# A three-block transformer kernel: merged orders in latent and memory attention, boundary sums of the last two tiles on TensorE

## The reference, cut to what matters

```python
# first block (x: 512 x 1024, mem: 256 x 1024)
y = hybrid_mixer(rms_norm(x, g1))                       # convolution + forgetting attention
x = x + rms_norm(y, g2)                                 # norm 1
q, k, v = rms_norm(x, g3) @ w_mq, mem_n @ w_mk, mem_n @ w_mv   # 4 heads of 128
y = (softmax(q @ k.T * 128 ** -0.5) @ v) @ w_mo         # memory attention
x = x + rms_norm(y, g4)                                 # norm 2
y = square(relu(rms_norm(x, g5) @ w_up)) @ w_down
x = x + rms_norm(y, g6)                                 # norm 3
# second block, two layers
c_q, c_kv, k_rope = split(x @ mla_w_in, [384, 256, 64])
q = rms_norm(c_q, g_q) @ w_uq                           # 8 heads, 128 plain + 64 rotated
k, v = split(rms_norm(c_kv, g_kv) @ w_ukv)
m = attention(q, k, v, rope) @ w_o                      # latent attention
x = layer_norm(alpha * x + m)                           # layer norm 1
x = layer_norm(alpha * x + conv_ffn(x))                 # layer norm 2
x = layer_norm(alpha * x + hyena_mixer(x))              # layer norm 3
x = layer_norm(alpha * x + conv_ffn(x))                 # layer norm 4, the output
```

## Time and profile before

| what | value |
|---|---|
| three runs | 2267.39, 2268.22, 2272.98 us |
| median | 2268.22 us |
| profiled execution | 2269.26 us |
| its span | 2267.5 us |
| mean granted TensorE clock | 0.949 of full speed |
| busy PE, DVE, POOL, ACT | 93%, 58%, 42%, 37% |

### The profile page before, as it was taken

The page is one execution under the profiler, slowest core; times in us unless marked ns, Lnnn a source line. Parts: engine busy times, 40 slices in busy tenths (PEclk is TensorE's granted clock), DMA queues, the critical chain, the costliest instruction groups (busy, mean ns, idle before and its releaser), DMA issues.

```text
span 2267.5 us, 23112 instructions
## 1 busy us (share of the span) xinstructions
PE 2113.5 (93%) x9481; PEld 1718.9 (76%) x9481; DVE 1323.7 (58%) x1597; ACT 840.9 (37%) x1194; POOL 941.4 (42%) x388
## 2 busy tenths in 40 slices
PE   8999989779999998899989999999988789999997
PEld 5777768668888886677778887877877677887786
DVE  7765871625234443455177776546578827777644
ACT  4623454453122224467143333223322324333322
POOL 4252145535444445111444444444666434444442
PEclk9998869889999998999989999999999989999998
DMA  5322112112232221111212222224231222222221
GB/s 196 136 97 74 38 38 89 62 54 75 97 108 93 93 93 54 40 48 38 75 56 95 104 98 93 93 74 160 91 129 52 110 73 75 93 96 98 104 93 38
DMA packets 34558, 194.02 MB, mean 86 GB/s; under 512 B 3903, under 2 KB 4495, under 8 KB 14932
## 3 DMA queue, kind: packets, MB, share of 16 engines
q1 hardware_dynamic: 34452, 192.54, 24.5%
HBM read 178.82 MB, written 13.64 MB: 85 GB/s over the span
## 4 chain that ended last, share of the span: by engine, by line
PE 61%; DVE 24%; ACT 10%; POOL 3%; issue 2%; DMA 0%; SPq 0%; DVEq 0%; POOLq 0%; ACTq 0%
PE ps L128 55%; DVE TMP L157 9%; DVE TMP L163 6%; PE ps L127 5%; ACT WH L144 4%; DVE TMP L151 1%; ACT TMP L145 1%; DVE X L151 1%; ACT PAD L144 1%; PE ps L136 1%; POOL X L151 1%; DVE ps L163 1%; DVE VG L151 1%; POOL WL L151 1%; POOL TMP L151 1%
## 5 line engine op out<-in xcount | busy, mean ns | idle before, releaser
L151 POOL TENSOR_TENSOR WL<-W,WH 128x2048 fp32r<-128x2048 f32 (+3 forms) x175 | 705.6, 4037 | 1036.4 <-ACT WH L144 1036.4
L128 PE MATMUL ps<-HH,WL 128*128 128x512 f32 x1456 | 583.9, 401 | 48.4 <-issue 15.6
L128 PE MATMUL ps<-HL,WH 128*128 128x512 f32 x1456 | 575.4, 395 | 0.0
L128 PE MATMUL ps<-HH,WH 128*128 128x512 f32 x1456 | 574.5, 395 | 0.0
L144 ACT ACTIVATE WH<-W 128x2048 fp32r<-128x2048 f32 (+2 forms) x157 | 291.8, 1859 | 322.5 <-PE ps L128 322.5
L128 PEld LDWEIGHTS ps<-HH,WL 128*128 128x128 f32 x1456 | 278.8, 192 | 120.8 <-issue 53.1
L128 PEld LDWEIGHTS ps<-HH,WH 128*128 128x128 f32 x1456 | 278.5, 191 | 60.2
L128 PEld LDWEIGHTS ps<-HL,WH 128*128 128x128 f32 x1456 | 279.0, 192 | 56.3 <-issue 0.2
L151 DVE TENSOR_TENSOR MRL<-MID,MRH 128x512 fp32r<-128x512 f32 x76 | 177.4, 2366 | 162.4 <-ACT MRH L144 162.4
L157 DVE TENSOR_SCALAR TMP<-PAD,PAR 128x512 f32<-128x512 f32 x88 | 209.0, 2375 | 69.9 <-ACT PAD L144 69.9
L128 PE MATMUL ps<-MRH,WL 128*128 128x512 f32 x608 | 238.3, 392 | 4.5 <-DVE TMP L163 2.3
(11 more groups left out here) (338 smaller groups left out, 3162.0 us busy)
## 6 DMA issues: line engine op xcount, KB each, us to landing
W<-in_up SPq DMA_DIRECT2D x44, 1024.0 KB, 4.8
W<-in_down SPq DMA_DIRECT2D x22, 1024.0 KB, 4.8
W<-in_w_up SPq DMA_DIRECT2D x16, 1024.0 KB, 4.8
W<-in_w_down SPq DMA_DIRECT2D x16, 1024.0 KB, 4.8
W<-in_hy_in SPq DMA_DIRECT2D x12, 1024.0 KB, 4.8
kd<-STG SPq DMA_DIRECT2D x36, 256.0 KB, 2.0
KB<-kd SPq DMA_DIRECT2D x8, 1024.0 KB, 5.1
W<-in_win_ag SPq DMA_DIRECT2D x4, 1024.0 KB, 4.8
```

The source lines that it names most:

```text
L128: return self.eng.matmul(out, lhs, rhs, start=start, stop=stop)
L151: return QUIET if self.eng is None else self.eng.tensor_tensor(out, a, b, op)
```

## The change

Memory attention: a second pair of buffers for the turned tiles; the heads overlap more in all three engines' lists; DVE does two of the four scalings. Latent attention: the sums of c_q and their spread come earlier in the input projection, the root and the high parts with them; low parts are made one tile late, so that the next scaling is not held up; the key/value scale is spread between query tiles; the swap stands ahead of the keys. Norms: POOL adds squares 0 to 5, and TensorE sums DG, square 6 and square 7; in norms 1 to 3 the scaled tiles 0 and 1 go to a PSUM bank (`yp`) instead of Y. Layer norms: the order of the sums is DG, square 6, X 7, square 7; HH 0 comes first and X 0 is scaled by DVE, which also makes HL 0; POOL makes HL 2, 4 and 5; mean and multiplication are interleaved between tiles. In layer norm 4 POOL subtracts and multiplies tiles 6 and 7 from copies of the two banks that ACT makes.

```diff
--- before.py
+++ after.py
@@ -339,8 +339,8 @@
...
         PM = [sb(f"PM{i}", A + (72, 88)[i], [128, 4, 256]) for i in range(2)]
-        PMH = sb("PMH", A + 92, [128, 2, 512], R)
-        PML = sb("PML", A + 96, [128, 2, 512], R)
+        PMH = [sb(f"PMH{i}", A + (92, 76)[i], [128, 2, 512], R) for i in range(2)]
+        PML = [sb(f"PML{i}", A + (96, 80)[i], [128, 2, 512], R) for i in range(2)]
         OMH = sb("OMH", A + 100, [128, 4, 512], R)
@@ -518,8 +518,8 @@
...
                                 ins = step(ps, m, k, wh, wl)
-                                if within and k == KT // 2:
-                                    within(g)
+                                if within:
+                                    within(g, k)
                             ins.then_inc(*up(acc, (group, g), *[("w_used", n)] * (m == MT - 1)))
@@ -719,7 +719,10 @@
...
             def post(s, name):
-                column_sum([(("ys", s), DG, ("yacc", s, 6), None, None),
+                reserve("yp", s)
+                close("yp", s)
+                column_sum([(("ys", s), DG, ("yacc", s, 5), None, None),
+                            (("ys", s), tmp(name, 6), ("ysq", s, 6), (name, 6), None),
                             (("ys", s), tmp(name, 7), ("ysq", s, 7), (name, 7), ("ys", s))])
@@ -775,7 +778,8 @@
...
                     pe.wait_ge(*at("vm", j))
-                    ins = pe.mm3(ps[:], VMH[:, j, blk(h)], VML[:, j, blk(h)], PMH[:, j, :], PML[:, j, :], j == 0, j == 1)
+                    ins = pe.mm3(ps[:], VMH[:, j, blk(h)], VML[:, j, blk(h)], PMH[h % 2][:, j, :], PML[h % 2][:, j, :],
+                                 j == 0, j == 1)
                 ins.then_inc(*up(acc, ("mo", h)))
@@ -785,13 +789,16 @@
...
             mem_t(0)
+            mem_s(2)
             mem_q(3)
-            for h in range(4):
-                if h < 2:
-                    mem_s(h + 2)
-                mem_pv(h)
-                if h < 3:
-                    mem_t(h + 1)
+            mem_t(1)
+            mem_pv(0)
+            mem_s(3)
+            mem_t(2)
+            mem_pv(1)
+            mem_pv(2)
+            mem_t(3)
+            mem_pv(3)
@@ -841,11 +848,11 @@
...
-            def within_in(n):
-                if n == 4:
+            def within_in(n, k):
+                if (n, k) == (4, 3):
                     column_sum([(("cqs",), DG, ("cqadd", 1), None, None),
                                 (("cqs",), tmp("cq", 2), ("cqsq", 2), ("cq", 2), ("cqs",))])
-                if n == 5:
+                if (n, k) == (5, 0):
                     spread("nq", slot=12)
@@ -864,6 +871,8 @@
...
                     ins.then_inc(*up(acc, ("uq", p, m), *[("w_used", n)] * (m == 2)))
+                    if p == 0 and m == 1:
+                        spread("nv", slot=20)
@@ -925,7 +934,6 @@
...
             mla_uq(0)
-            spread("nv", slot=20)
             swap_q(0)
@@ -936,8 +944,8 @@
...
                     mla_uq(p + 1)
+                    swap_q(p + 1)
                     mla_k(p + 1)
-                    swap_q(p + 1)
                 mla_t(2 * p + 1)
@@ -956,7 +964,9 @@
...
                 ds, dq = ("ds", d), ("dq", d)
-                column_sum([(ds, X[:, 7, :], ("cx", d, 7), None, ds), (dq, DG, ("qacc", d, 6), None, None),
+                column_sum([(dq, DG, ("qacc", d, 5), None, None),
+                            (dq, tmp("dc", d, 6), ("dcq", d, 6), ("dc", d, 6), None),
+                            (ds, X[:, 7, :], ("cx", d, 7), None, ds),
                             (dq, tmp("dc", d, 7), ("dcq", d, 7), ("dc", d, 7), dq)])
@@ -1354,7 +1364,7 @@
...
-                for i in range(4):
+                for i in range(2):
                     s, p = 32 * (h % 2) + 168 + i, PM[h % 2][:, i, :]
@@ -1362,9 +1372,9 @@
...
                     act.wait_ge(*at("mt", h, j))
-                    if h:
-                        act.wait_ge(*at("mo", h - 1))
-                    high(PMH[:, j, :], bank("mt", h, j)[:], ("pm", h, j))
+                    if h >= 2:
+                        act.wait_ge(*at("mo", h - 2))
+                    high(PMH[h % 2][:, j, :], bank("mt", h, j)[:], ("pm", h, j))
@@ -1379,15 +1389,18 @@
...
             mem_norm(1)
+            mem_exp(2)
             mq_high(3)
-            for h in range(4):
-                if h < 2:
-                    mem_exp(h + 2)
-                mem_out(h)
-                if h < 3:
-                    mem_turned(h + 1)
-                if h < 2:
-                    mem_norm(h + 2)
+            mem_norm(2)
+            mem_turned(1)
+            mem_out(0)
+            mem_exp(3)
+            mem_turned(2)
+            mem_norm(3)
+            mem_out(1)
+            mem_out(2)
+            mem_turned(3)
+            mem_out(3)
             roots_next()
@@ -1457,14 +1470,17 @@
...
                         act.copy(KRS[:], bank("mi", 0)[:]).then_inc(*out(("krs",)))
+                    if m == 3:
+                        root(("cqs",), 8, "eps6")
                     if m == 4:
-                        root(("cqs",), 8, "eps6")
-            for k in range(3):
-                q_high(k)
+                        q_high(0)
+                        q_high(1)
+            q_high(2)
+            weights(CH["uq"][0])
             root(("cvs",), 16, "eps6")
-            weights(CH["uq"][0] + 1)
             act.wait_ge(*at("rkt"))
             high(KRH[:], AN2[:], ("kr",))
+            weights(CH["uq"][0] + 1)
@@ -1489,11 +1505,11 @@
...
-            nope(0)
             query(0)
...
                 high(CVH[:, k, :], tmp("nv", k)[:], ("cvn", k))
+            nope(0)
@@ -1558,8 +1574,17 @@
...
                 act.act(SM[:, 24:28], SM[:, 24:28], ACT.Sqrt, 1.0, par("eps5")).then_inc(*out(("sd", d)))
+                if not split:
+                    act.wait_ge(*at("mu", d))
+                    act.copy(RS[:], bank("mu", d)[:]).then_inc(*out(("mus",)))
+                    act.wait_ge(*at("rstd", d))
+                    act.copy(DG[:], bank("rstd", d)[:]).then_inc(*out(("rstds",)))
                 for k in range(8):
                     act.wait_ge(*at("xn", d, k))
+                    if split and k == 0:
+                        act.act(HH[:, 0, :], X[:, 0, :], ACT.Identity, par(g), par(b)).then_inc(
+                            *out(("hn", 4 + d, 0, "hi")))
+                        continue
                     if split:
@@ -1955,16 +1980,22 @@
...
             def post(s, Y, g, g2):
+
                 inverse(("ys", s), 8, [("col", "rps", s)])
+                dve.wait_ge(*at("free", *earlier["yp", s]))
                 for k in range(10):
                     if k < 8:
+                        yn = Y[:, k, :] if k > 1 else bank("yp", s)[:]
                         dve.wait_ge(*at("rps", s))
                         dve.wait_ge(*at("y", s, k))
-                        dve.stt(Y[:, k, :], Y[:, k, :], par(g, k), bank("rps", s)[:], ALU.mult, ALU.mult).then_inc(
+                        if k == 1:
+                            dve.wait_ge(*at("xr", s, 0))
+                        dve.stt(yn, Y[:, k, :], par(g, k), bank("rps", s)[:], ALU.mult, ALU.mult).then_inc(
                             *out(("yn", s, k), *[("free", "rps", s)] * (k == 7)))
...
                         dve.wait_ge(*at("yn", s, k))
-                        dve.tt(X[:, k, :], X[:, k, :], Y[:, k, :], ALU.add).then_inc(*out(("xr", s, k)))
+                        dve.tt(X[:, k, :], X[:, k, :], yn, ALU.add).then_inc(
+                            *out(("xr", s, k), *[("free", "yp", s)] * k))
                     else:
@@ -2002,10 +2033,18 @@
...
                 dve.recip(SM[:, s + 8:s + 12], SM[:, s + 4:s + 8]).then_inc(*out(("rcp", "ms_", h)))
+                dve.wait_ge(*at("rcp", "ms_", h))
+                for i in (2, 3):
+                    p = PM[h % 2][:, i, :]
+                    dve.ts(p, p, SM[:, s + 8 + i:s + 9 + i], None, ALU.mult).then_inc(*out(("mp", h, i)))
...
                 for j in range(2):
-                    low(PML[:, j, :], bank("mt", h, j)[:], PMH[:, j, :], ("pm", h, j), ("free", "mt", h, j))
+                    low(PML[h % 2][:, j, :], bank("mt", h, j)[:], PMH[h % 2][:, j, :], ("pm", h, j),
+                        ("free", "mt", h, j))
+
+            def mem_out(h):
+                low(OML[:, h, :], bank("mo", h)[:], OMH[:, h, :], ("om", h), ("free", "mo", h))
@@ -2017,13 +2056,16 @@
...
             mem_low(0)
+            mem_soft(2)
             mq_out(3)
-            for h in range(4):
-                if h < 2:
-                    mem_soft(h + 2)
-                low(OML[:, h, :], bank("mo", h)[:], OMH[:, h, :], ("om", h), ("free", "mo", h))
-                if h < 3:
-                    mem_low(h + 1)
+            mem_low(1)
+            mem_out(0)
+            mem_soft(3)
+            mem_low(2)
+            mem_out(1)
+            mem_out(2)
+            mem_low(3)
+            mem_out(3)
             post(2, Y2, "g_mem_post", "g_mlp_pre")
@@ -2061,7 +2103,14 @@
...
```

(63 more changed lines are left out.)

## The result

| kernel | median (runs) | ratio to the kernel before | 95% interval |
|---|---|---|---|
| before, beside it | 2267.84 us (4) | | |
| changed, first time | 2254.39 us (4) | 0.9934 | 0.9917 to 0.9952 |
| changed, second time (label e5_after_again) | 2254.73 us (6) | 0.9945 | 0.9928 to 0.9962 |

By the medians the change takes 13.4 us off the first time and 11.4 the second (2266.11 beside it), by the ratios 15.0 and 12.5 (0.0066 and 0.0055 x 2268). Forecast were 8.8, and the first time lies 0.1 us under the low end of the range.

What follows compares the result with a forecast made beforehand. TensorE, busy 93% of the span, was taken as the bound, so only its work and waits count; terms 0 - 1.0 - 1.9 - 0.3 - 5.5 - 2.3 + 2.2 + 0 = -8.8 gave a 2259.4 us median, range 2254.5 to 2265.5.

Steps and rivals of the forecast that it cites:

- Norm 2: Second norm: GpSimd's shorter sums and first tiles in PSUM let TensorE start sooner, until GpSimd's chain limits it; -1.9 us.
- the entry: Latent attention up to the first product with QR: earlier root and spread, fewer waits, less half clock; -5.5 us.
- the end: After the last spread in layer norm 4: final tiles shared with GpSimd, ACT's last copy sooner; -1.8 us.
- layer norm 2: Eight more sums on TensorE at half clock, though GpSimd was not late; +1.7 us in the sum.
- The signs named for the trace: Expected marks: HL 0 about 4.8 us behind the spread, QR waits gone, 0.8 on QRS, layer norm 2 sums about 7.
- memory: Memory attention: second turned-tile buffers and shared scalings shorten each head, but new waits appear; -1.0 us, bounds -3.8 and +1.5.
- norm 3: Third norm: sums all at half clock, last tiles wait for HL 6 and 7 behind GpSimd's adds; -0.3 us.
- pairs: Latent attention's three pairs: swap ahead of keys replaces QR waits with shorter QRS waits; -2.3 us, bounds -0.5 and -3.5.
- the layer norms: Layer norms 1 to 4: extra tile summed on TensorE costs +0.3, +1.7, +0.2; at the fourth +1.78 against -1.8, 0.
- (b): Rival: denser feeding holds 2.4 GHz through the sums, so layer norms 2 and 4 cost less; 2255.8 us, chance 0.12.
- (a): Rival: waits at the latent attention's start, its pairs and memory attention are replaced, not removed; 2265.2 us, chance 0.22.
- (c): Rival: one-column sums run at half clock at every norm and layer norm, kernel slower; 2271.6 us, chance 0.05.

Runs made afterwards that it cites:

- e5_after_again: The changed kernel, all groups of edits together against the kernel before, measured a second time: 2254.73 us (6 runs), ratio 0.9945.
- the kernel before with the wait: Kernel before, with GpSimd's cut of the first full w_up chunk after norm 2 waiting for VectorE's seventh square-add: 2265.95 us, ratio 0.9994.
- latent attention alone: Kernel before with only the latent attention's edits, input projection and pairs: 2258.82 us, ratio 0.9964.
- memory taken back: Changed kernel with the memory attention's edits undone: 2258.64 us, ratio 0.9960.

## Why the prediction was off, step by step

**Right in kind and nearly in size.** Norm 2 (-1.9, found -2.1), the entry (-5.5, found -5.7 alone and -6.6 over all), the end (-1.8, found -1.7), layer norm 2 (+1.7, found +1.3). The signs named for the trace came: HL 0 4.80 us behind the spread, waits of 0.69 to 0.78 on QRS, none of 1.4 for QR, half clock gone from 941 to 947. The sums before layer norm 2 took 6.4 us where about 7 were named.

**Mis-sized, and all the same way: memory, norm 3, pairs.** Together these three terms are 3.6 us short, and two steps of the forecast failed in them.

The first is the price of the memory attention. The forecast laid out 2.8 us of waiting at query 3 and 3.9 ahead of the product of head 2, and took the difference of the waits as the gain (-1.0). Query 3 came as laid out (3.12), but the wait at head 2 was 1.13 to 2.38, with 1.14 more at head 3, and the stretch lost 2.3 us on the mean. It is the softmax chain that got shorter by this, and the waits of TensorE, which also depend on its clock, do not measure it.

The second is that at norm 3 and at the pairs the clock was left as it was. At norm 3 the forecast held the sums to be at half clock for good (3.55 for 16 in the earlier trace rows). In five traces they took 2.81 to 3.69 us for 24, and the stretch 187.6 to 188.5 us, 2 to 3 under the 190.6 of before. In the other five they took 4.84 to 5.25, mostly at half clock, and the stretch 189.6 to 190.0, 0.6 to 1 under it. At the pairs the waits gave 2.7 instead of 2.3, and the half-clock stretch behind the third pair, worth 1.2, was gone in nine of twelve traces. The forecast did this sum only at the entry, and there the size held partly by luck: it put the stretch at 941 to 947 at about 3 us, and the one trace of the old entry without half clock between 925 and 950 (the kernel before with the wait) took 63.57, only 1.8 less.

The other deviations nearly cancel: norm 1 -0.5, norm 2 -0.2, w_up +2.0, entry -1.1, layer norms -0.1, end +0.1.

**Missing: the collision.** The forecast let VectorE and TensorE gain 2 us at norm 2 and asked what GpSimd's chain would do to HL, but not what else VectorE had queued behind: the adds for the next norm's sum, 0.1 us clear of GpSimd's next cut. +2.0 on the mean, +4.2 in the profiled execution. By luck it hid part of the error above: without it the total would have been some 2 us further off. The port pair had been considered, but only for the first tiles' gain.
The Trainium skill, "SBUF — State Buffer", section "Who interferes with whom", says that a VectorE instruction with two SBUF inputs contends with a GpSimd instruction that reads SBUF, that the shared ports are an exclusive lock, and that the order of issue decides who is blocked. The rows agree: the add was held to 0.55 us behind the cut's end.

**Wrong reason at the layer norms.** The sums cost 1.7, 1.3, 1.7 and 0.1 (forecast 0.3, 1.8, 0.2, 1.8): nearly the same sum, other places. The idle 0.72 us was to be filled by the new sums; it stands as before, now ahead of them ([0.72 <-DVE X] at 1112.17). VectorE's X is no input of that sum; by the code it is its read that frees a PSUM bank, which was not tried. At the fourth the stretch grew by 0.1 only: in the kernel before the clock fell at 2248.2, inside the last sixteen sums (2.92 us), in the changed kernel only at 2234.4, at their end. The forecast had put the eight more there at half clock.

**The rivals.** (b) gave 2255.8, the nearest to the time, but not by what happened: at layer norm 2 the clock fell in the sums as before.
The Trainium skill, "TensorE: Matmul & The Clock Gate", part 1, lays half clock to idling alone. The trace contradicts it at 1504, where the clock was half and TensorE had been busy without a pause since 1499.8.
(a) did not occur at any of its places. (c), one-column sums at half clock everywhere, is out: 24 in 2.81 us at norm 2.

## What to carry over

Ask first which engine sets the end of a stretch: where another engine's chain does, as in the memory attention, lay out that chain and not TensorE's waits. Elsewhere, price a wait that an edit removes with the half-clock stretch that follows it, or give both values, and take the clock from several traces: one differs from the next by 3 us in code that nobody touched. When an edit makes a chain of one engine earlier, list the other instructions of VectorE with two SBUF inputs and of GpSimd around it and their distances; a distance of tenths can fall either way, as it did in four traces with the same code up to there. Don't give the bounding engine more work where the engine that is relieved was not late: undoing that here made the fastest version.

## What the hardware did that was not expected

- A 128x512 add of two SBUF tiles on VectorE, 0.73 us otherwise, took 5 us when it began just behind a GpSimd operation of 4.56 us. The other way round little was lost: GpSimd's cut that began 0.1 us ahead of the end of an add took 4.58, and in two traces (latent attention alone, memory taken back), where it began 0.4 ahead, 4.87 and 4.86.
- A faster TensorE made the kernel slower for 180 us: in the kernel with the layer norms' edits alone the clock returned about 1.3 us sooner behind norm 2, where nothing was changed, and w_up took 3 us more.
- The same first 350 us of code took 346.97 to 352.91 in the eighteen traces.
- From the scores of head 3 to w_mo 12.84 to 12.88 us passed in ten traces, whether 3.1 or 6.0 us of them were at half clock.
